# Two kinds of sums in a hybrid decoder kernel: products of rounded parts in place of fp32 products, and decays laid out earlier

## What is computed

```
qh = l2_norm(heads(q)) * HEAD_DIM ** -0.5      # l2_norm(x) = x * rsqrt(sum(x*x) + EPS)
kh = l2_norm(heads(k))
beta = sigmoid(b_in)
g = -exp(A_log) * softplus(a + dt_bias)
g_cum = cumsum(g)                              # in each chunk of 64 tokens
decay = exp(where(causal, g_cum[..., :, None] - g_cum[..., None, :], -inf))
lower = where(strict, einsum(k * beta, k) * decay, 0)
attn_intra = where(causal, einsum(q, k) * decay, 0)
... # a triangular solve with I + lower, then a scan over the chunks
```

## Time and profile before

| | before |
|---|---|
| median of 3 runs | 2092.49 us (2092.34 to 2092.87) |
| the profiled execution, its own time | 2092.73 us |
| span in the profile | 2090.9 us |
| PE busy | 2074.3 us, 99% of the span |
| DVE busy | 1027.8 us, 49% |
| ACT busy | 774.6 us, 37% |
| POOL busy | 380.4 us, 18% |

### The profile page before, as it was taken

One profiled execution on the slowest core, in us unless ns is written; L12 is line 12 of the kernel. 1 busy time (PEld: TensorE's weight loads), 2 busy tenths in 40 slices (PEclk: granted clock), 3 DMA queues, 4 the chain that ended last, 5 costly groups with the idle time before them and its releaser, 6 DMA issues.

```text
span 2090.9 us, 31663 instructions
## 1 busy us (share of the span) xinstructions
PE 2074.3 (99%) x13097; PEld 1678.5 (80%) x13097; DVE 1027.8 (49%) x1391; ACT 774.6 (37%) x1058; POOL 380.4 (18%) x343
## 2 busy tenths in 40 slices
PE   9999999999999999999999999999999999999999
PEld 7888888877777888888888888888777778888887
DVE  5433333588775643333333443336887765343322
ACT  5222222475556422222232222224755554222211
POOL 1010011205034511001111110111050444101000
PEclk9999999999999999999999999999999999999999
DMA  5222222322121222222222222223212112222222
GB/s 194 88 98 100 96 91 96 122 81 82 43 92 39 99 86 99 100 96 91 99 99 100 100 92 90 104 82 136 81 63 74 61 61 81 100 100 97 92 98 76
DMA packets 30645, 192.40 MB, mean 92 GB/s; under 512 B 3216, under 2 KB 5392, under 8 KB 11984
## 3 DMA queue, kind: packets, MB, share of 16 engines
q1 hardware_dynamic: 30160, 189.80, 26.0%
q10 hardware_dynamic: 384, 1.14, 0.1%
HBM read 188.70 MB, written 2.10 MB: 91 GB/s over the span
## 4 chain that ended last, share of the span: by engine, by line
PE 89%; DVE 6%; ACT 3%; issue 1%; POOL 1%; DMA 0%; SPq 0%; DVEq 0%; ACTq 0%; POOLq 0%
PE psum L995 28%; PE psum L997 27%; PE psum L996 27%; PE psum L1475 1%; PE psum L1425 1%; DVE wl L1916 1%; PE psum L1442 1%; ACT wh L1542 1%; PE psum L1313 1%; PE psum L1310 1%; DVE wrk L2014 1%; DVE XL L1931 1%; DVE m L2012 1%; DMA raw<-weights 0%; PE psum L1131 0%
## 5 line engine op out<-in xcount | busy, mean ns | idle before, releaser
L995 PE MATMUL psum<-XH,wh 128*128 128x512 f32 x1904 | 754.9, 396 | 5.6 <-DVE XL L1876 2.3
L997 PE MATMUL psum<-XH,wl 128*128 128x512 f32 x1904 | 742.3, 390 | 0.0
L996 PE MATMUL psum<-XL,wh 128*128 128x512 f32 x1904 | 742.2, 390 | 0.0
L995 PEld LDWEIGHTS psum<-XH,wh 128*128 128x128 f32 x1904 | 357.5, 188 | 102.0 <-issue 22.4
L997 PEld LDWEIGHTS psum<-XH,wl 128*128 128x128 f32 x1904 | 357.6, 188 | 74.9
L996 PEld LDWEIGHTS psum<-XL,wh 128*128 128x128 f32 x1904 | 357.8, 188 | 71.6 <-issue 1.0
L1924 DVE TENSOR_TENSOR wl<-raw,wh 128x2048 fp32r<-128x2048 f32 x88 | 201.8, 2293 | 159.4 <-ACT wh L1547 159.4
L1542 ACT ACTIVATE wh<-raw 128x2048 fp32r<-128x2048 f32 (+1 forms) x88 | 161.6, 1836 | 305.2 <-PE psum L997 305.0
L995 PE MATMUL psum<-HH,wh 128*128 128x512 f32 x704 | 274.1, 389 | 0.0
L996 PE MATMUL psum<-HL,wh 128*128 128x512 f32 x704 | 274.0, 389 | 0.0
L997 PE MATMUL psum<-HH,wl 128*128 128x512 f32 x704 | 274.0, 389 | 0.0
(11 more groups left out here) (255 smaller groups left out, 1939.7 us busy)
## 6 DMA issues: line engine op xcount, KB each, us to landing
raw<-weights SPq DMA_DIRECT2D x143, 1024.0 KB, 4.8
raw<-weights SPq DMA_DIRECT2D x32, 896.0 KB, 4.4
xT<-xt SPq DMA_DIRECT2D x4, 512.0 KB, 6.2
memT<-memt SPq DMA_DIRECT2D x2, 1024.0 KB, 4.8
out<-xT SPq DMA_DIRECT2D x8, 256.0 KB, 5.0
stripsA<-strip_table SPq DMA_DIRECT2D x2, 768.0 KB, 6.7
raw<-weights SPq DMA_DIRECT2D x2, 512.0 KB, 6.7
stripsB<-strip_table SPq DMA_DIRECT2D x2, 512.0 KB, 7.3
```

Of the source, the lines that this page charges most:

```text
L995: pe.matmul(out_ap, a_hi, b_hi, start=first, stop=False)
L996: pe.matmul(out_ap, a_hi, b_lo, start=False, stop=False)
L997: return pe.matmul(out_ap, a_lo, b_hi, start=False, stop=last)
```

## The change

The sums of groups 4 and 5 (`SPLIT`), and the four sums of decays in each layer, are no longer one fp32 product each. The moving operand is split into a rounded part and the rest, the weights (zeros and ones) are copied to the rounded type, and two fp32r products are added in PSUM.

- ACT: copies `same64` to `same_r` once a layer and squares groups 4 and 5 a second time, into `sq_hi`.
- POOL: subtracts `sq_hi` from `nsq` to get `sq_lo` (twice a layer); copies `suffix` to `suffix_r`; lays out `TG_hi` and `TG_lo` (eight instructions for four). It no longer waits for the memory's v to be copied before it starts on them, only for `acc_done` 24; before `LT` it now waits for `nq_r` 6.
- DVE: two small instructions behind `gdec` split it into `g_hi` and `g_lo`.
- PE: two products for one, in the same places.
- The new tiles lie over others whose use is past; four semaphores become counters that go on over the layers.

The diff, without the tiles and the semaphore counters:

```diff
@@ pool
                         elif kind == "rows":
-                            pool.wait_ge(S["ev_act"], copied(GROUP_AT["mv", 1])[1])
                             pool.wait_ge(S["acc_done"], 24)
+                            pool.tensor_copy(suffix_r[:, :], const("suffix"))
                             for b in range(NB):
-                                g = gdec[:, b, :].rearrange("p (c a) -> p a c", a=2)
-                                pool.tensor_tensor(TG[:, b].rearrange("p (a c) d -> p a c d", a=2),
-                                                   const("upper64").unsqueeze(1).unsqueeze(1).to_broadcast([P, 2, 3, DH]),
-                                                   g.unsqueeze(3).to_broadcast([P, 2, 3, DH]), ALU.mult
-                                                   ).then_inc(S["tg_done"], 1)
+                                for dst, part in ((TG_hi, g_hi), (TG_lo, g_lo)):
+                                    g = part[:, b, :].rearrange("p (c a) -> p a c", a=2)
+                                    ins = pool.tensor_tensor(dst[:, b].rearrange("p (a c) d -> p a c d", a=2),
+                                                             const("upper64").unsqueeze(1).unsqueeze(1).to_broadcast([P, 2, 3, DH]),
+                                                             g.unsqueeze(3).to_broadcast([P, 2, 3, DH]), ALU.mult)
+                                ins.then_inc(S["tg_done"], 1)
+                            pool.wait_ge(S["nq_r"], SPLIT[-1] + 1)
...
+                        elif step[0] == "sq" and step[1] in SPLIT:
+                            nth_sum = 1 + SPLIT.index(step[1])
+                            pool.wait_ge(S["nq_sq"], step[1] + 1)
+                            pool.wait_ge(S["hs_hi"], of("hs_hi", nth_sum))
+                            pool.tensor_tensor(sq_lo[step[1] % 2][:, :], nsq[step[1] % 2][:, :],
+                                               sq_hi[step[1] % 2][:, :].bitcast(F32), ALU.subtract
+                                               ).then_inc(S["hs_lo"], 1)
@@ tensor, head_sums
+                        if nj in SPLIT:
+                            pe.wait_ge(S["hs_lo"], of("hs_lo", 1 + SPLIT.index(nj)))
+                            pe.matmul(bank[2 + nj % 2][:, 0:n], same_r[:, :], sq_hi[nj % 2][:, :], start=True, stop=False)
+                            pe.matmul(bank[2 + nj % 2][:, 0:n], same_r[:, :], sq_lo[nj % 2][:, :],
+                                      start=False, stop=True).then_inc(S["nq_ss"], 1)
+                            return
@@ tensor, decay
-                            pe.matmul(bank[pb][:, 0:WB], const("suffix"), TG[:, b].rearrange("p h c -> p (h c)"),
-                                      start=True, stop=True).then_inc(S["dt_ps"], 1)
+                            pe.matmul(bank[pb][:, 0:WB], suffix_r[:, :], TG_hi[:, b].rearrange("p h c -> p (h c)"),
+                                      start=True, stop=False)
+                            pe.matmul(bank[pb][:, 0:WB], suffix_r[:, :], TG_lo[:, b].rearrange("p h c -> p (h c)"),
+                                      start=False, stop=True).then_inc(S["dt_ps"], 1)
@@ scalar, square_of
+                        if nj in SPLIT:
+                            if nj == SPLIT[0]:
+                                act.activation(same_r[:, :], const("same64"), ACT.Copy)
+                            act.activation(sq_hi[nj % 2][:, :], src, ACT.Square).then_inc(S["hs_hi"], 1)
@@ vector, gate3
                             dve.sem_inc(S["g_ready"], 1)
+                            chain.step(dve.tensor_copy(g_hi.bitcast(F32R), gdec))
+                            chain.join()
+                            chain.step(dve.tensor_tensor(g_lo, gdec, g_hi, ALU.subtract))
```

More of the change, by code:

```diff
@@ L445 @@
                   os_ps=4, os_read=4, or_done=4, op_done=4, jr_done=N_BATCHES, jo_done=N_BATCHES, jx_done=N_BATCHES, jb_done=N_BATCHES, og_done=4, gh_done=3, gl_done=3, cb_done=18, tap_done=9, pr_done=24, ex_done=16, hf_hi=3, hf_lo=3,
-                  sm_t=1, sp_e=1, sp_b=1, g_ready=1)
+                  sm_t=1, sp_e=1, sp_b=1, g_ready=1, hs_hi=2, hs_lo=2, row_ps=1, mem_ps=1)
+SPLIT = (4, 5)
 def nth(b, j):
@@ L586 @@
 LAYER_SEMAPHORES = """
-cv_zero mem_in mem_sq mem_s mem_ps mem_r mem_hi mem_lo strip_in unsel_done
+cv_zero mem_in mem_sq mem_s mem_r mem_hi mem_lo strip_in unsel_done
 pj_done ev_act ev_dve sc_done relu_done acc_done
 nq_sq nq_ss nq_r nq_done conv_done silu_done
-v_t v_done gc_ready row_ps row_ready
+v_t v_done gc_ready row_ready
 jl_done jm_done je_done jtr_done jp_even jp_odd jv_done
@@ L658, in hybrid_trunk @@
         beta, gdec, bg, kdec, tmpa, tmpb, tmpc = (gcol[:, i] for i in range(7))
+        g_hi, g_lo = tmpb, tmpc
         m8 = sb("m8", [P, 8])
@@ L687, in hybrid_trunk @@
             ML = sb("ML", [P, KD, NM], F32R, first)
-            memT = sb("memT", [P, KD, NM], F32, first)
+            with ExitStack() as early:
+                memT = sb("memT", [P, KD, NM], F32, early)
+            sq_hi, sq_lo = ([sb(f"sq_{n}{i}", [P, T], F32R, first) for i in range(2)] for n in ("hi", "lo"))
             iqT = sb("iqT", [P, 2, T], F32, first)
@@ L693, in hybrid_trunk @@
             memrow = sb("memrow", [P, NM], F32, first)
-            nsqm = sb("nsqm", [P, NM], F32, first)
+            with ExitStack() as early:
+                nsqm = sb("nsqm", [P, NM], F32, early)
+            same_r = sb("same_r", [P, P], F32R, first)
         FT = sb("FT", [P, NB, H_B, DH])
@@ L702, in hybrid_trunk @@
         EGl = sb("EGl", [P, 3, 2 * NB])
-        with ExitStack() as early:
-            TG = sb("TG", [P, NB, H_B, DH], F32, early)
         XTF = sb("XTF", [P, NB, H_B, DH])
@@ L721, in hybrid_trunk @@
         WT = sb("WT", [P, NB, 3, P])
+        with ExitStack() as early:
+            TG_hi = sb("TG_hi", [P, NB, H_B, DH], F32R, early)
         AT = sb("AT", [P, NB, H_B, DH])
+        with ExitStack() as early:
+            TG_lo = sb("TG_lo", [P, NB, H_B, DH], F32R, early)
         kdc = sb("kdc", [P, NB, WB])
+        with ExitStack() as early:
+            suffix_r = sb("suffix_r", [P, P], F32R, early)
         stripsC = sb("stripsC", [P, 1, T])
@@ L1673, in small_step @@
                         elif kind == "mem4":
-                            act.wait_ge(S["mem_ps"], 1)
+                            act.wait_ge(S["mem_ps"], of("mem_ps", 1))
                             chain.step(rsqrt(memrow[:, :], bank[6][:, 0:NM], 1.0 / D))
@@ L1697, in small_step @@
                         elif kind == "gate7":
-                            act.wait_ge(S["row_ps"], 1)
+                            act.wait_ge(S["row_ps"], of("row_ps", 1))
                             act.activation(rowg[0:GROWS, :], bank[2][0:GROWS, :], ACT.Copy).then_inc(S["row_ready"], 1)
```

## The result

The changed kernel takes 2098.72 us, the median of 11 runs (2097.32 to 2100.39), against 2092.8 us for the kernel before beside it (11 runs, 2092.34 to 2093.49). The ratio is 1.0027, with a 95% interval of 1.002 to 1.0035: slower by 0.27%. The forecast was 2098.0.

The account below looks back on a forecast made before the run. ACT and DVE, not the 99% busy PE, were taken to set the pace where the sums stand. 0.3 + 1.25 + 0.4 + 0.8 = 2.75 us a layer, 5.5 for two, gave 2098.0 us; range 2093.5 to 2101.0 (80%).

Parts of the forecast that it names:

- PE's 4 us: Shorter sums of squares and decays on PE, 4.0 us together; counted as nothing, since ACT and DVE end the waits behind.
- The gate split: Two small DVE instructions behind gdec delay the copy into cv at 407.69: 0.3 us a layer (0.1 to 0.5).
- The table load: ACT's table load for silu at 467.44, waiting for the copy of z, comes 1.25 us late a layer (0.3 to 1.7).
- the held sum: DVE's first index sum, ready at 463.66, is held by POOL's subtractions until 464.4: 0.75 us.
- the squares in ACT's queue: Second squares and a copy delay ACT's relus by 1.25 us; after 0.77 to spare, the table load is 0.5 late.
- `wl` against `TG`: POOL's TG holds DVE's wl in the chain, due at 476.1, until 476.5: 0.4 us a layer (0 to 0.8).
- The products with k against `LT`: POOL's four LT start where DVE's two products with k stand and hold them: 0.8 us a layer (0 to 1.4).
- Behind 504 all differences stay constant: Sign expected in the changed profile: from 504 us to the end of the layer, lateness no longer changes.
- engines do not hold each other off: Rival: only queue delays stay, 0.3 + 0.5 us a layer, 2094.1 us; partial collisions up to 2096.7; chance 22%.
- all is hidden: Rival: table load and copy into cv wait for something later, so PE only waits longer; 2092.5 us, chance 8%.
- PE sets the pace: Rival: PE decides in the touched stretches and its 4.0 us gain shows; 2088.5 us, chance 4%.
- A table load between rounded and plain outputs: Rival: ACT's rounded copy or square takes 1.28 us table loads each way; 2103 us, 8% with other large surprises.

Follow-up runs that it names:

- one product: Kernel before, with one rounded product per decay sum in place of the fp32 product, low half left out; 2093.49 us against 2093.11.
- all clear: Changed kernel, with rounded squares behind the last relus, gate split on GpSimd, and GpSimd's subtractions, TG and LT placed later; 2093.74 us, kernel before 2093.16.
- no low squares: Changed kernel without GpSimd's two sq_lo subtractions, both products of a sum reading sq_hi (sums come out wrong); 2096.94 us, kernel before 2093.11.
- `LT` late: Changed kernel with GpSimd's four LT held back until the copy of the memory's v; 2096.76 us, kernel before 2093.19.
- gap filled: Changed kernel with seven idle products of 512 columns on TensorE in its gap of 1.94 us; 2098.02 us, kernel before 2093.16.
- DVE lightened: Decays alone split, additions moved away, 14 of 16 replacements of one selection left out (output wrong); 2089.02 us, kernel before 2093.01.

## Why the prediction was right

- **That PE's 4 us count for nothing.** Shown by one product, by all clear and by the rows of layer 1, but for the 0.28 us at 524.82, which stand in no forecast.
- **The gate split, 0.3.** Measured 0.22 at PE (the wait for `cv` is 0.42 in place of 0.19).
- **The table load, 1.25.** 1.65 late in all; less the gate's share, which is 0.26 there, 1.39. Its two parts are shown apart: 0.94 for the held sum (forecast 0.75; no low squares), and 0.45 for the squares in ACT's queue (forecast 0.5). The held sum was the assumption without a row, and the mechanism came as forecast; the 0.94 are more than the 0.75 since `sq_lo` started 0.3 us later than worked out. By the rule of the Trainium skill (SBUF — State Buffer, section "SBUF: two separate sides") a VectorE instruction with two inputs in SBUF and a GpSimd instruction that reads SBUF exclude each other, and whoever starts first keeps the ports to its end; by that rule the trace agrees, with 4.27 us for 3.33.
- **`wl` against `TG`, 0.4.** 0.30, and only in company with the squares.
- **The products with k against `LT`, 0.8.** 0.63, where `LT` late is 0.70 earlier.
- **The sum, 2.75 a layer.** 0.22 + 1.39 + 0.30 + 0.63 = 2.54; 2.60 measured at the gap of layer 0. 5.1 to 5.2 in two layers; with full clock the kernel is 4.9 slower (gap filled), with its usual clock 5.9.
- **Two things that the prediction had not.** The clock adds some 0.7 to 1.1 us. And "Behind 504 all differences stay constant" is not quite so: at 524.82 the lateness goes from 4.37 to 4.09, since the wait of 0.22 us before is absent there. The forecast of 2098.0 is 0.7 under the median, and that it came so near is in part luck, since errors of both signs meet: the clock adds 0.7 to 1.1 and the kernel before ran 0.3 higher beside it than in the times shown first, less these 0.28 and the 0.2 a layer by which the sum was too high.
- **The rivals.** That engines do not hold each other off fails by three rows (4.27, 2.59, 1.92) and by the runs that took each away. That all is hidden fails by the gap, and that PE sets the pace by the time itself, by one product and by all clear. A table load between rounded and plain outputs does not occur in ACT's rows. The rounded pair is faster than the fp32 product (1.08 us for 1.88), so that rival is out too.

## What to carry to other kernels

A faster instruction on an engine that is 99% busy can be worth nothing where it stands in front of a wait; look at which wait ends last behind it, and test it cheaply by leaving the work out, as with one product here. What pays for the faster form (rounding, splitting, copies) runs on the engines that everyone waits for, and a queue is a place as much as a price: the same additions cost 5.9 us in one order and 0.6, which is not told from nothing, in another. When GpSimd gets work early "because it is free then", list the VectorE instructions with two inputs in SBUF that fall into that time; each may be held for one GpSimd instruction.

## What the runs showed of the hardware

- VectorE and GpSimd hold each other off in both directions where the VectorE instruction has two inputs in SBUF (4.27 us for 3.33 one way, 2.88 for 0.83 the other), and a small instruction waits as long as a large one: with the gate split on GpSimd, a copy of 24 columns took 2.26 us, until `wl` ended (timeline of POOL, all clear).

```profile
468.43 2.26 POOL L870 CAST gcol<-gcol 128x24 fp32r<-128x24 f32 x1
470.63 0.29 POOL L871 CAST suffix_r<-cst 128x128 fp32r<-128x128 f32 x1
```

- A gap of 1.94 us on TensorE, with two of 0.61 and 0.69 in the 12 us before it, was followed by a fall of its granted clock to the 1.2 GHz level, in some executions and not in others, and with idle products in the gap no execution of nine had a fall. The first 15 us of an execution can have one too, in about a quarter of the executions of the kernel before, by their mean clock.
- A PE that is busy for all of a stretch by its records (17.80 of 17.80 us) need not set the pace there: 1.9 us a layer less of its work gave nothing (one product), and with the decays split and DVE lightened PE is again busy for all 17.80 us, at 2 us less a layer.
